# First stage of a hybrid decoder trunk: norm sums block by block, other order of transfers and of ScalarE's and VectorE's work

## The reference, cut to what matters

```python
def rmsnorm(x, g):
    y = xf * lax.rsqrt(jnp.mean(xf * xf, axis=-1, keepdims=True) + EPS)
    return (y * g.astype(jnp.float32)).astype(x.dtype)

def modulate(x, g, shift, scale):
    return rmsnorm(x, g) * (1 + scale[:, None, :]) + shift[:, None, :]

mods = (jax.nn.silu(c) @ w_ada + b_ada).reshape(B, N_MOD, D_MODEL)   # N_MOD = 16, D_MODEL = 1024
h = modulate(x, norm_g[l, 0], m[:, 0], m[:, 1])
a = h @ w_pw1 + b_pw1
u = a[..., :D_MODEL] * jax.nn.sigmoid(a[..., D_MODEL:])
up = jnp.concatenate([prev.astype(u.dtype), u], axis=1)              # prev: state_conv for the samples
y = depthwise convolution of width 31 over up, + b_dw; LayerNorm; silu; @ w_pw2
```

## Time and profile before

| | us |
|---|---|
| median of 3 runs | 1669.32 |
| lowest, highest | 1665.81, 1680.36 |
| the profiled execution | 1672.92 |
| its span, first to last instruction | 1671.3 |
| TensorE, VectorE, ScalarE, GpSimd busy | 1557.1, 1124.4, 778.7, 220.1 |

### The profile page before, as it was taken

One profiled execution on the slowest core, in us unless ns is written; L12 is line 12 of the kernel. 1 busy time (PEld: TensorE's weight loads), 2 busy tenths in 40 slices (PEclk: granted clock), 3 DMA queues, 4 the chain that ended last, 5 costly groups with the idle time before them and its releaser, 6 DMA issues.

```text
span 1671.3 us, 34581 instructions
## 1 busy us (share of the span) xinstructions
PE 1557.1 (93%) x13797; PEld 1407.8 (84%) x13797; DVE 1124.4 (67%) x2277; ACT 778.7 (47%) x1646; POOL 220.1 (13%) x325
## 2 busy tenths in 40 slices
PE   5898999999999999989999899889899999999996
PEld 3887868889999999989999554555799999999995
DVE  5899957785757758683362667556368585875765
ACT  4554666543534525442224655445245353452534
POOL 2016240000000110102001444243000000000000
PEclk8999999999999999999999999788999999999998
DMA  9989873145436554524223400110331332433221
GB/s 326 285 289 309 288 183 102 51 117 149 131 124 187 164 137 127 135 80 114 69 66 106 120 26 1 52 47 7 90 88 51 109 81 72 110 89 97 77 76 57
DMA packets 237948, 200.11 MB, mean 120 GB/s; under 512 B 8082, under 2 KB 196834, under 8 KB 237520
## 3 DMA queue, kind: packets, MB, share of 16 engines
q1 hardware_dynamic: 222192, 156.52, 31.9%
q0 software_dynamic: 7376, 25.59, 5.3%
q10 hardware_dynamic: 8224, 15.83, 2.9%
HBM read 188.87 MB, written 11.20 MB: 120 GB/s over the span
## 4 chain that ended last, share of the span: by engine, by line
PE 70%; DVE 12%; issue 7%; ACT 5%; DMA 3%; POOL 1%; DVEq 1%; ACTq 0%; SPq 0%; POOLq 0%
PE ps L2292 28%; PE ps L2619 24%; PE ps L2272 4%; PE ps L2343 4%; PE ps L2744 2%; PE ps L2791 2%; PE ps L2672 2%; DMA raw<-in_ffn_w_up_dram 1%; DVE wl L1485 1%; DVE y L1782 1%; DVE r L1782 1%; PE ps L2308 1%; DMA xrows<-in_x_sample_dram 1%; DVE t L1553 1%; PE ps L2861 1%
## 5 line engine op out<-in xcount | busy, mean ns | idle before, releaser
L870 ACT ACTIVATE wh<-raw 128x1024 fp32r<-128x1024 f32 (+2 forms) x129 | 118.6, 922 | 276.9 <-PE ps L2292 249.4
L2619 PE MATMUL ps<-Hh,bh 128*128 128x288 f32 x608 | 180.3, 297 | 3.3 <-ACT Z L1223 1.9
L2619 PE MATMUL ps<-Hh,bl 128*128 128x288 f32 x608 | 179.1, 295 | 0.0
L2619 PE MATMUL ps<-Hl,bh 128*128 128x288 f32 x608 | 179.0, 294 | 0.0
L2292 PE MATMUL ps<-Hh,wh 128*128 128x288 f32 (+1 forms) x688 | 152.6, 303 | 8.3 <-DVE t L1957 3.6
L1485 DVE TENSOR_TENSOR wl<-raw,wh 128x1024 fp32r<-128x1024 f32 (+2 forms) x129 | 135.4, 1050 | 20.5 <-ACT wh L870 20.0
L2292 PE MATMUL ps<-Hh,wl 128*128 128x288 f32 (+1 forms) x688 | 148.3, 297 | 0.0
L2292 PE MATMUL ps<-Hl,wh 128*128 128x288 f32 (+1 forms) x688 | 148.2, 297 | 0.0
L2292 PE MATMUL ps<-ah,wh 128*128 128x288 f32 x656 | 141.1, 297 | 1.8 <-issue 1.8
L2292 PE MATMUL ps<-ah,wl 128*128 128x288 f32 x656 | 140.5, 296 | 0.0
L2292 PE MATMUL ps<-al,wh 128*128 128x288 f32 x656 | 140.4, 296 | 0.0
(11 more groups left out here) (393 smaller groups left out, 3912.2 us busy)
## 6 DMA issues: line engine op xcount, KB each, us to landing
ada<-in_w_ada_dram SPq DMA_DIRECT2D x49, 1024.0 KB, 8.4
raw<-in_ffn_w_up_dram SPq DMA_DIRECT2D x88, 512.0 KB, 4.9
ada<-in_w_ada_dram ACTq DMA_DIRECT2D x15, 1024.0 KB, 8.8
raw<-in_conv_w_pw_dram SPq DMA_DIRECT2D x24, 512.0 KB, 9.8
raw<-in_ffn_w_down_dram SPq DMA_DIRECT2D x32, 384.0 KB, 3.9
raw<-in_ffn_w_down_dram SPq DMA_DIRECT2D x32, 320.0 KB, 3.2
raw<-in_w_kv_dram SPq DMA_DIRECT2D x12, 512.0 KB, 4.1
out_win_sample_dram<-in_state_win_dram POOLq DMA_DIRECT2D x8, 512.0 KB, 3.8
```

The lines of the kernel that those rows point to most:

```text
L870: A(wh[:, u % RING, 0:K, 0:w], raw[:, u % RING, 0:K, 0:w], ACT.Copy).then_inc(hi_ready, 1)
L2619: last = M(ps[:, bank, 0:HT], wt[:, blk, k], rt, start=(j in (0, 1, 2, 6) and k == 0 and i == 0), stop=(k == 3 and i == 2), skip_group_che ...
```

## The change

x leads the transfers: blocks 1 to 4 go out on SP's queue ahead of the strips, block 0 on ScalarE's, and the tables that ScalarE issued are now GpSimd's. The order of the strips is scale, shift, scale, shift (`ORDER` 2, 0, 3, 1), a fourth buffer `ada_x` lets the first four halves go out at once, and the weight tiles 0 and 1 are issued behind two halves instead of four. The sums of the first norm are made per block of x: one square over 8 chunks of 128 columns, one plain addition of chunks 0 to 3 and 4 to 7, four products with the ones, and a root and a reciprocal per block; the root's table is loaded ahead. The scaled chunks go to a buffer of their own (`Hs`, all chunks) and are made as soon as the scale is there (`scaled0`), the shift last (`shifted0`). The 16 tap row copies are spread in four groups (`tap_rows`). The first two tap tiles are VectorE's. The state rows are loaded one half later, transposed behind the first pass, and copied behind the sigmoid, ahead of high part 3.

```diff
-ORDER = [0, 2, 1, 3] + list(range(4, N_STRIP))
+ORDER = [2, 0, 3, 1] + list(range(4, N_STRIP))
...
 sp.dma_start(ident[:], c["ident"]).then_inc(S("id_in"), 16)
+sp.dma_start(rows0[0:8, 4, :], ...).then_inc(S("c_in"), 16)
+sp.dma_start(rows0[8:72, 4, :], ...).then_inc(S("c_in"), 16)
+for bk in range(1, 5):
+    load_rows(sp, bk)
...
-            strips(4)
+            strips(2)
             unit()
             unit()
             strips(8)
...
-            pool.wait_ge(lo_ready, 2)
-            for j in range(2):
-                nc.gpsimd.tensor_tensor(taps4[:, j % 2], sel32[:]..., wd4[:, :, :, j:j + 1]..., ALU.mult)
-            pool.wait_ge(ada_used, 2 * STRIPS_FIRST - 1)
+            pool.wait_ge(ada_used, 2 * STRIPS_FIRST)
             for bk in range(5, 7):
-                load_rows(bk)
+                load_rows(pool, bk)
...
+            A(scrap[:], epst[:], ACT.Sqrt).then_inc(S("st_tb"), 1)
             for bk in range(5):
                 block_out(bk)
+                square0(bk)
+                if bk >= 2:
+                    root0(bk - 2)
+            root0(3)
+            root0(4)
...
+            strip_out(2, None)
+            strip_out(None, 2)
             strip_out(3, None)
-            norm0_hi(3)
             strip_out(None, 3)
-            split_hi(2)
             norm0_smp(1)
             for cc in range(4, DC):
                 norm0_hi(cc)
-            for h in range(2):
-                block_out(5, h)
+            split_hi(2)
...
                     if u == 1:
-                        split_hi(3)
+                        for h in range(2):
+                            block_out(5, h)
                         strip_out(s_, None)
                         for h in range(2):
                             block_out(6, h)
+                        split_hi(3)
...
+            scaled0(0)
+            split_lo(0)
+            split_lo(1)
+            dve.wait_ge(S("wd4"), 1)
+            V.tensor_reduce(sel32[:], ...)
+            tap_rows(0)
+            shifted0(0)
+            scaled0(1)
+            tap_rows(1)
+            tap_rows(2)
+            shifted0(1)
             split_lo(2)
+            tap_rows(3)
+            dve.wait_ge(S("vec_dve"), 8)
+            for j in range(2):
+                V.tensor_tensor(taps4[:, j], sel32[:]..., wd4[:, :, :, j:j + 1]..., ALU.mult)
...
             def first_strips(k):
                 if k == 1:
+                    strip_half(2, 1)
+                elif k == 3:
+                    turn_strip(2)
+                    strip_half(3, 0)
+                elif k == 4:
                     strip_half(3, 1)
                     turn_strip(3)
-                elif k == 4:
-                    block_in(5)
-                elif k == 6:
-                    strip_half(4, 0)
...
             dense(0, Hh, Hl, normed0, tiles=2, ahead=first_strips)
+            block_in(5)
+            strip_half(4, 0)
             strip_half(4, 1)
             block_in(6)
```

More of the change, by code:

```diff
@@ L182, with _ada_slots @@
 RING_ADA = 3
+FIRST_HALVES = 2 * STRIPS_FIRST
+def _ada_slots():
+    out = []
+    for n in range(2 * N_STRIP):
+        if n < FIRST_HALVES:
+            out.append(n % (RING_ADA + 1))
+        elif n < ADA_LATE:
+            out.append((n - FIRST_HALVES) % RING_ADA)
+        else:
+            out.append((n - ADA_LATE + 1) % 2)
+    return out
+ADA_SLOT = _ada_slots()
+ADA_NTH = [ADA_SLOT[:n + 1].count(ADA_SLOT[n]) for n in range(2 * N_STRIP)]
+ADA_PRIOR = [max([m for m in range(n) if ADA_SLOT[m] == ADA_SLOT[n]], default=-1) for n in range(2 * N_STRIP)]
 PROMPTS = [(0, 1), (0, 3), (1, 3), (1, 1), (2, 1), (0, 2), (2, 3), (0, 0),
@@ L491, in build @@
         tile_done, tile_free = S("tile_done"), S("tile_free")
[L492 removed]
+        ada_in = [S(f"ada_in{i}") for i in range(RING_ADA + 1)]
         pair_in = [S(f"pair_in{i}") for i in range(2)]
@@ L1686, in _ @@
+            for bk in range(2, 5):
+                inverse0(bk)
             dve.wait_ge(S("xi_act"), 5)
```

273 lines of the change are left out of this document (132 added, 141 removed).

## The result

| | before | after |
|---|---|---|
| median of 20 runs each, side by side | 1671.99 us (1665.81 to 1680.36) | 1682.46 us (1675.64 to 1686.84) |
| ratio after/before | | 1.0058 [1.0044, 1.0073] |
| profiled execution, its span, mean granted clock | 1672.92, 1671.3, 0.974 | 1685.75, 1684.1, 0.963 |

Slower, by 10 us. The forecast was 1674.3 (1665 to 1681): right in direction, half the size. Of the distance of 8.2 us, 2.7 are the base, since the 20 runs of before have a median that much above the three it started from. The other 5.5 come mostly from behind the first stage.

The account below looks back on a forecast made before the run. VectorE's convolution was taken to bind from 60 to 200 us, so the tap loop's start counts: 71.4 against 65.84, 5.6 us later, taken as 5.0 for overlap. Added to the median 1669.32, this gave 1674.3 us, range 1665 to 1681.

Parts of the forecast that it names:

- k=0: First step of TensorE's first dense pass: forecast to start at 34.6 us instead of 40.93.
- VectorE's own queue: Head of the stage: VectorE's work ahead of the shift lasts until 32.4 us and sets when k=0 starts.
- the gap of 4.07 us: First pass, ahead of k=4: TensorE idle for 4.8 us while VectorE prepares the second four chunks.
- the half clock behind it: TensorE after the idle gap: clock falls to half for 4.8 us, so 2.4 us are lost.
- Rival A: TensorE's clock stays up through the gap: 2.4 us less, +2.6 us, 1671.9 us; chance 0.20.
- Rival B: Not slower: early sums, TensorE keeps full clock from its first transposes, loop 1.9 us earlier, 1667.4 us; chance 0.18.
- the strip's bound of 29.8: Head: rows for the shift of the first four chunks, from half 3 of the strips, ready at 29.8 us.
- the tail: First sigmoid to tap loop: 10.95 us instead of 5.93, high part 3 behind four copies; costs 5.0 us.
- Rival C: State rows land late, 3 us more, and everything behind the sigmoid waits: +8 us, 1677.3 us; chance 0.10.
- Rival D: Change does not reach the end: transfers or TensorE bind later in the convolution; 0, 1669.3 us; chance 0.07.
- at least 1.3 us: End of the convolution: of each microsecond the loop starts earlier, at least 1.3 us in all reach the end, by ScalarE's idle time.
- goes whole to the end: Tap loop to program end: every microsecond of later loop start passes on in full; 5.0 us taken.

Follow-up runs that it names:

- e6: The changed kernel with 26 matmul instructions of ones filling TensorE's idle gap ahead of k=4 of the first pass; 1681.95 us, ratio 1.0046.
- e7: The changed kernel with modulation-row halves 5 to 7 and their turns earlier in the pass, and tap row copies 1 and 2 behind the second shift add; 1673.83 us, ratio 0.9999.
- e1: The changed kernel with high parts 3 and 4 right behind the sigmoid, ahead of the state rows' copies; 1680.40 us, ratio 1.0028.
- e2: The kernel before with only the new tail (state rows transposed behind the pass, copied ahead of high part 3); 1678.45 us, ratio 1.0021.
- e4: The kernel before with eight more computations of the second tap on VectorE ahead of the loop, a pure delay; 1677.32 us, ratio 0.9998.
- e10: e7 with the old tail: block 5's transposes and half 8 back inside the first pass, block 5's copies ahead of the sigmoid; 1672.20 us, ratio 0.9993.
- e14: e10 with the late modulation-row halves in the same buffers as in the kernel before; 1671.35 us, ratio 0.9990.
- e16: e14 with 47 small matmuls of ones (188 instructions) added behind turn 0, to move TensorE's code fetches; 1672.88 us, ratio 0.9979.
- e17: The kernel before with 17 small matmuls of ones (68 instructions) added ahead of half 3 of the modulation rows; 1669.38 us, ratio 0.9965.
- e8: e7 with the reordering of e1, and the first u_s row copies ahead of the row of strip 5; 1679.57 us, ratio 1.0051.
- e5: The changed kernel unaltered, timed again beside new runs of before; 1680.36 us, ratio 1.0040.
- e18: The changed kernel with 47 small matmuls of ones (188 instructions) added behind turn 0, to move TensorE's code fetches; 1677.43 us, ratio 1.0015.
- e11: e8 with 26 matmuls of ones added behind turn 0, where TensorE waits for half 2; 1676.66 us, ratio 1.0019.

## Why the prediction was right and wrong

**Right in the number, by another path: k=0.** It starts at 34.01 (forecast 34.6). The forecast had VectorE's own queue as the last thing there, ready for the shift at 32.4, and the shift's rows at 29.8. It was the other way round: VectorE was done with the work ahead of the shift by 29.1 and idle for 2.53 us, until the rows were there at 31.6. Two errors of 1.8 us and 3.3 us left a number that was right by luck. Behind it the mechanism is right: the gap of 4.07 us (4.8), as k=4 waits for VectorE, and the half clock behind it (0.50 granted, lifted by filling in e6). The time lost to it was forecast from a slow stretch "that began with k=0 at 40.93"; the granted clock had been at 0.50 since 35.5. Rival A had no support: the clock fell. Rival B was right that TensorE's transposes start early (6.3) and that VectorE's queue then ends near 29.6, and wrong on the strip's bound of 29.8, the gap and the clock. e7 shows what B needed.

**Right: the tail.** 10.54 us from sigmoid to loop (10.95), with the copies ahead of high part 3 as its cause (e1: the wait of 4.79 goes). Alone it costs 2.6 at the loop (e2) and not 4.6, because the pass ahead of it gets 2.0 us shorter; the forecast has that in its time for the sigmoid, not in the tail's 5.0.

**Right in size: the loop and the convolution's end.** Loop 3.6 and 5.2 us late (5.0), end 5.4 and 5.1 late; e4 passed on 3.4 of 4.1. The loop of 69.45 is just ahead of the 70 to 71.5 that was named as a sign, and in that profile the end owes 1.8 us to the sigmoids of the last two blocks. The forecast took 205.3 us for the last of the GLU; that is the seventh block's, and the eighth's comes at 220.56, behind a wait of 3.2 us for its sigmoid that the forecast's window up to 215 us left out. Rival C: the state rows landed by 55.8 and were transposed from 58.7, in time. Rival D, 0: wrong for a delay. For a gain it depends on the next sigmoid: in e7, e10, e14, e16 and e17 the gain at the loop reaches the end whole or nearly (2.0 of 2.0, 4.5 of 4.1, 5.9 of 6.1, 3.9 of 4.1, 3.0 of 3.0), in e1 and e8 it is gone at sigmoid 1, since their copies hold up TensorE's second pass. The forecast's "at least 1.3 us" of a gain comes from ScalarE's idle time at 205 and says nothing of that wait.

**Wrong: what comes behind.** The step that failed is that a delay "goes whole to the end", with which the sum moved the whole rest of the program as one block: a span later by 5.0 us, nothing added. The delay grew instead, by 2.1 to 2.4 us at 350 us (0.4 of it a later start of VectorE behind a landed transfer, up to 0.6 of transfer, 1.5 of half clock behind it) and, through a fetch of TensorE's code inside an awaited transfer, by 1.5 to 1.6 us at 1308. With the 5.4 and 5.1 us at the convolution's end that makes 9.4 and 8.7 us; measured by the medians are 10.5 and 6.8. So the two terms that the sum put at nothing are 3.6 to 4.0 of the 5.5 us that were missing behind the first stage. What is left, +1.1 in one group and -1.9 in the other, is as large as the scatter. The cause of the step at 1308 is shown, that of the half clock at 350 is in part argued.

The clock is, for the most part, in this account already and not a third term. Over the first 35 runs of before, which are the same program, the time follows TensorE's time at half clock, counted as 2(1 - clock) x time, with 0.33 us per us and a correlation of 0.92 (0.29 to 0.38 in the other groups). In the group of e5 the 12 runs of after have 106 us of it, the 35 of before 94. But in the profiles the extra lies ahead of 226 us (20.5 us before, 44.4 and 37.6 in the two of after) and at 350 (0 and 3.4), where it is part of the delays above; from 420 to 1200 us the two have 57 and 48, before 51, which is scatter in both directions. e18's runs have as little half clock as those of before (96 us both), and its ratio, 1.0015 [0.9993, 1.0038], is below that of after by more than the 1.6 us of the step that it takes out; how much of that is the clock can't be said.

**The base.** The sum was added to the median of three runs, which more runs raised by 2.7 us; the range had 4 us for that, and nothing for a delay that grows behind the change.

## What to carry to other kernels

Look in the order of the prologue for the transpose or turn that the second half waits for, and place it as early as its transfer allows, with copies that nobody needs yet behind it: together that was worth 6.5 us here (e7 against e5). A gain ahead of a long stretch bound by one engine passes on only if the next thing that this engine waits for comes earlier too: sigmoid 1 did in e14 (79.6, before 84.9), and not in e1 and e8 (86.3 and 85.7). Before moving work in front of a wait on a transfer, see what is queued behind it (e8). And when the time differs by half a per cent, lay two profiles of each kernel side by side along the whole program: a change in the first 60 us can cost at 350 and 1308 us.

## What was not expected of the hardware

TensorE's code is fetched by DMA throughout (16 KB, about 1 us, one per 255 of its instructions), and a fetch inside a short awaited transfer made it land 2 us later. In e6 and e11 TensorE stood still for 2.9 and 2.3 us at such a fetch, with nothing else to wait for. A fp32 matmul that is written once was two matmul instructions and two weight loads. TensorE's clock, not the work, makes most of the scatter between executions of this kernel, and 34 matmul instructions of nothing in a wait of 3 us gave a faster kernel than the change did.
